# A two-block transformer on one core: weights' buffers moved by 64 bytes, later layers' inputs laid out 1024 bytes apart per feature tile

## The reference, cut to what matters

```
n = rmsnorm(h); proj = n @ w_in                       # qkv, iq, ak, av, aq, gates, z
merged = sig(gate_a) * (y_gdn @ w_branch_gdn) + sig(gate_b) * (y_dsa @ w_branch_dsa)
h = h + rmsnorm(merged @ w_out)
h = h + rmsnorm(square(relu(rmsnorm(h) @ w_up)) @ w_down)
x = x + rmsnorm(retention(rmsnorm(x), a_w_in, a_w_out))
x = x + rmsnorm((silu(g) * u) @ w_down0)              # [g, u] = conv3(rmsnorm(x) @ w_up0)
k, v = rmsnorm(x) @ w_kv
x = x + rmsnorm(diff_attention(rmsnorm(x), k, v, w_q, ...))
x = x + rmsnorm((silu(g) * u) @ w_down1)
```

## Time and profile before

| | us |
|---|---|
| median of three runs | 1258.31 |
| the profiled execution | 1258.36 |
| its span in the trace | 1256.6 |
| TensorE busy | 1240.9 |
| VectorE busy | 920.2 |
| ScalarE busy | 698.9 |
| granted clock of TensorE, mean | 0.998 of full speed |

### The profile page before, as it was taken

One profiled execution on the slowest core, in us unless ns is written; L12 is line 12 of the kernel. 1 busy time (PEld: TensorE's weight loads), 2 busy tenths in 40 slices (PEclk: granted clock), 3 DMA queues, 4 the chain that ended last, 5 costly groups with the idle time before them and its releaser, 6 DMA issues.

```text
span 1256.6 us, 23318 instructions
## 1 busy us (share of the span) xinstructions
PE 1240.9 (99%) x9036; PEld 1163.5 (93%) x9036; DVE 920.2 (73%) x1294; ACT 698.9 (56%) x1082; POOL 166.0 (13%) x113
## 2 busy tenths in 40 slices
PE   8999999999999999999999999999999999999998
PEld 7997999999989998889998989999889998999986
DVE  8786874878768775457734557999758777999954
ACT  6556465654446443445354646666557567766652
POOL 0000142000000000000000001663200000465310
PEclk9999999999999999999999999999999999999999
DMA  8452333311365545555553455545565444455562
GB/s 319 162 175 101 135 135 101 135 68 68 140 213 185 191 177 201 191 179 185 182 208 111 149 186 168 195 173 198 193 227 176 161 153 166 168 178 189 183 238 98
DMA packets 30316, 212.46 MB, mean 169 GB/s; under 512 B 3488, under 2 KB 3616, under 8 KB 5280
## 3 DMA queue, kind: packets, MB, share of 16 engines
q1 hardware_dynamic: 29088, 206.15, 46.9%
q0 software_dynamic: 1152, 5.24, 1.2%
HBM read 210.33 MB, written 1.05 MB: 168 GB/s over the span
## 4 chain that ended last, share of the span: by engine, by line
PE 90%; DVE 6%; ACT 3%; issue 1%; DMA 0%; DVEq 0%; SPq 0%; ACTq 0%
PE lin L541 52%; PE lin L707 21%; PE lin L568 2%; PE lin L2928 2%; DVE wlo L514 1%; PE lin L570 1%; ACT whi L507 1%; PE aux L2672 1%; PE aux L2644 1%; PE aux L730 1%; PE lin L2351 1%; PE aux L2530 1%; PE aux L2790 1%; PE aux L2600 1%; PE aux L2476 0%
## 5 line engine op out<-in xcount | busy, mean ns | idle before, releaser
L514 DVE TENSOR_TENSOR wlo<-raw,whi 128x2048 fp32r<-128x2048 f32 x183 | 424.6, 2323 | 163.4 <-ACT whi L507 162.8
L507 ACT CAST whi<-raw 128x2048 fp32r<-128x2048 f32 x192 | 365.1, 1905 | 175.4 <-DMA raw<-in_stream 145.8
L541 PE MATMUL lin<-xhi,whi 128*128 128x256 f32 (+2 forms) x1584 | 451.1, 285 | 1.9 <-DVE ctmp L1657 1.9
L541 PE MATMUL lin<-xlo,whi 128*128 128x256 f32 (+2 forms) x1584 | 447.3, 282 | 0.0
L541 PE MATMUL lin<-xhi,wlo 128*128 128x256 f32 (+2 forms) x1584 | 446.8, 282 | 0.0
L541 PEld LDWEIGHTS lin<-xhi,whi 128*128 128x128 f32 x1584 | 299.8, 189 | 3.7 <-issue 2.5
L541 PEld LDWEIGHTS lin<-xhi,wlo 128*128 128x128 f32 x1584 | 300.0, 189 | 0.0
L541 PEld LDWEIGHTS lin<-xlo,whi 128*128 128x128 f32 x1584 | 298.4, 188 | 0.4
L871 POOL TENSOR_TENSOR fu<-fs,ft 128x256 f32<-128x256 f32 x44 | 98.8, 2246 | 258.3 <-ACT fs L1485 258.3
L2311 DVE SCALAR_TENSOR_TENSOR ft<-fy,par,ft 128x254 f32<-128x254 f32 (+1 forms) x176 | 112.4, 678 | 5.9 <-DVE ft L2311 0.2
L541 PE MATMUL lin<-whi,xhi 128*128 128x256 f32 x256 | 73.9, 289 | 0.0
(11 more groups left out here) (463 smaller groups left out, 2163.3 us busy)
## 6 DMA issues: line engine op xcount, KB each, us to landing
raw<-in_stream SPq DMA_DIRECT2D x192, 1024.0 KB, 4.9
gp<-in_gains POOLq DMA_DIRECT2D x6, 512.0 KB, 3.9
c<-in_const SPq DMA_DIRECT2D x1, 1460.0 KB, 15.6
h<-in_x SPq DMA_DIRECT2D x2, 544.0 KB, 4.2
c<-in_const POOLq DMA_DIRECT2D x1, 1024.0 KB, 6.6
ht<-in_xtok POOLq DMA_DIRECT2D x1, 1024.0 KB, 9.7
raw<-in_stream SPq DMA_DIRECT2D x1, 640.0 KB, 6.4
out<-ht SPq DMA_DIRECT2D x1, 512.0 KB, 2.6
```

The costliest lines, as they stand in the source:

```text
L507: nc.scalar.copy(whi[:, s0 % 4], raw[:, s0 % 4]).then_inc(hi_ready, 1)
L514: nc.vector.tensor_tensor(wlo[:, s0 % 4], raw[:, s0 % 4], whi[:, s0 % 4].bitcast(F32), ALU.subtract).then_inc(lo_ready, 1)
L541: ins = nc.tensor.matmul(out, a, b, start=start and n == 0, stop=stop and n == 2)
```

## The change

The weights' buffers begin 64 bytes later. `ones` moves up behind them; nine small tensors become slices of one tensor `few` without padding, so that everything behind ends 128 bytes earlier than before (B is 93056). From the end of the first block's mixing on, the inputs of a layer no longer use the 272-column tiles: `xs_of` has for each of the five layer boundaries its own view of the same place, with 256 columns per tile (1024 bytes) and its own start, XAT bytes further on. No instruction is added or taken away, and no wait.

```diff
+WAT = 64
+XAT = {"mlp": 0, "ret": 64, "ffn0": 64, "diff": 0, "ffn1": 128}
...
-        raw = at("raw", 0, [P, RAW_N, KT, NCOL])
-        wlo = at("wlo", 0, [P, RAW_N, KT, NCOL], F32R)
-        whi = at("whi", 32768, [P, RAW_N, KT, NCOL], F32R)
-        par = at("par", 65536, [P, NPAR])
-        cursor = [65536 + 4 * NPAR]
+        raw = at("raw", WAT, [P, RAW_N, KT, NCOL])
+        wlo = at("wlo", WAT, [P, RAW_N, KT, NCOL], F32R)
+        whi = at("whi", WAT + 32768, [P, RAW_N, KT, NCOL], F32R)
+        ones = at("ones", WAT + 65536, [P, P])
+        par = at("par", WAT + 66048, [P, NPAR])
+        cursor = [WAT + 66048 + 4 * NPAR]
...
-        ones = nxt("ones", [P, P])
-        eps = nxt("eps", [P, 3])
+        few = nxt("few", [P, 75])
+        eps, gcum, ktsc, rcol = few[:, 0:3], few[:, 3:20], few[:, 20:29], few[:, 29:31]
+        ss, bs, rc, s2 = few[:, 31:35], few[:, 35:37], few[:, 37:39], few[:, 39:41]
+        bcg = few[:, 41:75].rearrange("p (n c) -> p n c", c=17)
...
         xhi = at("xhi", B, [P, KT, T1], F32R)
         xlo = at("xlo", B + 8704, [P, KT, T1], F32R)
+        xs_of = {name: tuple(at(f"{part}_{name}", B + 8704 * n + o, [P, KT, SEQ], F32R) for n, part in enumerate(("xhi", "xlo")))
+                 for name, o in XAT.items()}
...
-                nc.scalar.activation(xhi[:, kt, c * P:c * P + P], turned_tile(kt, c), ACT.Copy,
+                nc.scalar.activation(xs_of[pre][0][:, kt, c * P:c * P + P], turned_tile(kt, c), ACT.Copy,
...
-            pe_post_layer(pe, "wout", xhi, xlo, "mlo", KT, lambda end: end // 2, pre="mlp")
-            pe_layer("up", xhi[:, :, 0:SEQ], xlo[:, :, 0:SEQ], lead=4, pre="mlp")
+            pe_post_layer(pe, "wout", *xs_of["mlp"], "mlo", KT, lambda end: end // 2, pre="mlp")
+            pe_layer("up", *xs_of["mlp"], lead=4, pre="mlp")
...
-            x_hi, x_lo = xhi[:, :, 0:SEQ], xlo[:, :, 0:SEQ]
+            x_hi, x_lo = xs_of["ret"]
...
-                xh, xl = (x2hi, x2lo) if name == "dq" else (x_hi, x_lo)
+                xh, xl = (x2hi, x2lo) if name == "dq" else xs_of["diff"]
...
-            pe_layer(f"fu{k}", xhi[:, :, 0:SEQ], xlo[:, :, 0:SEQ], lead=2, pre=f"ffn{k}")
+            pe_layer(f"fu{k}", *xs_of[f"ffn{k}"], lead=2, pre=f"ffn{k}")
```

More of the change, by code:

```diff
@@ L171, in program @@
         gtmp = nxt("gtmp", [P, 3, 3, 8])
-        bcg = nxt("bcg", [P, 2, 17])
-        gcum = nxt("gcum", [P, 17])
-        ktsc = nxt("ktsc", [P, 9])
         egl = nxt("egl", [P, 8])
@@ L183, in program @@
         rstd = nxt("rstd", [P, T1])
[L184 to L188, removed]
         gqn = nxt("gqn", [P, 2, 8])
@@ L1026, in act_body @@
                     act.wait_ge(S("merged"), j + 1)
-                    nc.scalar.copy(xhi[:, 2 * j:2 * j + 2, 0:SEQ], merged[:, 2 * j:2 * j + 2]).then_inc(S("mhi"), 1)
+                    nc.scalar.copy(xs_of["mlp"][0][:, 2 * j:2 * j + 2], merged[:, 2 * j:2 * j + 2]).then_inc(S("mhi"), 1)
                     load_hi(FIRST[name] + j + 3, 0)
@@ L1552, in low @@
                 a = slice(c * P, c * P + P)
-                nc.vector.scalar_tensor_tensor(xlo[:, kt, a], turned_tile(kt, c), pcol(PRE_GAIN[pre], kt),
-                                               xhi[:, kt, a].bitcast(F32), ALU.mult, ALU.subtract)\
+                nc.vector.scalar_tensor_tensor(xs_of[pre][1][:, kt, a], turned_tile(kt, c), pcol(PRE_GAIN[pre], kt),
+                                               xs_of[pre][0][:, kt, a].bitcast(F32), ALU.mult, ALU.subtract)\
                     .then_inc(S("xlo"), 1)
@@ L1825, in dve_body @@
                 dve.wait_ge(S("mhi"), j + 1)
-                nc.vector.tensor_tensor(xlo[:, a, 0:SEQ], merged[:, a], xhi[:, a, 0:SEQ].bitcast(F32), ALU.subtract)\
+                nc.vector.tensor_tensor(xs_of["mlp"][1][:, a], merged[:, a], xs_of["mlp"][0][:, a].bitcast(F32), ALU.subtract)\
                     .then_inc(S("mlo"), 1)
@@ L2935, in out_part @@
                     ins.then_inc(S("tile_postdiff"), 1)
-            pe_token_pair("diff", x_hi, x_lo)
+            pe_token_pair("diff", *xs_of["diff"])
             project("dk", 0)
```

## The result

The changed kernel took 1263.91 us (six runs, 1260.82 to 1265.74) against 1258.37 (six runs of the kernel before, 1256.81 to 1258.65): ratio 1.0043, 95% interval 1.0033 to 1.0053. It is slower by 5.5 us; the forecast was 8.6 us faster. The profiled execution of after took 1265.74 us (span 1263.9), 7.3 us of span more than the one of before, and it is also the slowest of the six.

A forecast was written before the change was run, and what follows sets the result against it. TensorE was taken as the bound, its time a count of matmuls times a pace. Terms −1.4 − 2.5 − 1.2 − 3.0 − 0.5 = −8.6 us took the median 1258.31 to 1249.8; range 1238 to 1262, forecast's own 1243 to 1255.

The forecast's parts named there:

- the one on 512 columns: Six 512-column layers, M−S to 192: all at 226.7 ns, 0 for 1200 matmuls and −0.5 us for `wout`.
- the nearer row: Timeline row of `down`, 512 columns at constant M−S 0, 226.7 ns; taken as the pace at 192.
- its four rows: Timeline paces of `up` 118.3, `dq` 120.0, `down` 226.7 and `wout` 231.7 ns, said to differ only in operand places.
- Rival 3: 512-column layers stall at M−S 192: 1256.3 us, or 1261.9 at 236 ns; chance 0.13 for 1255 to 1262.
- rival 1: Evenly spaced 256-column layers settle at 120.0 ns, +7.3 us, total 1265; chance 0.13 for 1262 to 1265.
- M−S 128: `rq`, `rk`, `rv`, `rg`, `ret`'s token pair and `fu0`: from 118.3 to 117.5 ns, −0.8 ns a matmul.
- `fu1` at 192: 1008 matmuls of `fu1` go to 113.3 ns; with VectorE limiting, −3.0 us instead of the whole 5.0.
- the 240 matmuls at 192: Stationary-input matmuls in `dv` and the tiled slot of `up`: −5.0 ns each, −1.2 us.
- rival 4: Throughout the kernel distance does nothing and paces come from something else: 1258.4 us, chance 0.09.
- M−S 64: `wbd`, `wbg`, `dq` from 120.0 to 117.5 ns, −1.4 us; `up` beyond its tiled slot and `dk` from 118.3 to 117.5.
- The cap by VectorE in `fu1`: At 113.3 ns a `fu1` slot takes TensorE 5.44 us but VectorE 5.61, limiting the gain to −3.0 us.
- the free lag: In `fu1` VectorE may fall up to 2.5 us behind, 0.17 a slot, before TensorE waits; ten slots taken.

The follow-up runs named there:

- the first two experiments: Two variants of the changed kernel: M−S of 512-column layers back to 0, inputs' distances kept, 1254.72 us; inputs left 1088 bytes apart, 1263.67 us.
- the first experiment: Changed kernel with B padded so M−S of most 512-column layers is 0 again, XAT raised by 64 to keep the inputs' distances; 1254.72 us.
- the fifth kernel: Changed kernel with B padded so most 512-column layers stand at M−S 0, and XAT 192 for all inputs; 1249.71 us, ratio 0.9938.

## Why the prediction was wrong

**The step that failed** is the one on 512 columns: "I take 226.7 for all, the nearer row: it too has one distance throughout, and 192 is the one that did best with 256 columns." Its terms were 0 and −0.5 us; these layers measured +7.6 and +0.4. That is 8.5 us of the 14 between forecast and result. The nearer row was near in its tile spacing and not in M−S, the very quantity that the argument had just named; and a ranking from 256 columns was carried to 512, where it is turned round: 0 is best (226.7) and 192 worst (233.3). The prediction had called the place of the operands the one thing in which its four rows differ; they differ in columns as well. Rival 3 came true, with "From 233.3 on it eats the whole gain": all six layers came to 233.3 to 233.4. That the total, 1263.9, lies in the band of rival 1 (1262 to 1265) and above that of rival 3 is chance: of rival 1 only `rq` and `rk` at 120.0 came, and rival 3 had reckoned with the full gain of the other layers.

**The three smaller misses.** M−S 128 was taken at 117.5 from six matmuls in a row; where a layer stays there it settles at 118.7 or at 120.0: +1.2 us over 2160 matmuls instead of −1.7. (The caution in rival 1, that six may be too few, held for this distance.) `fu1` at 192 settled at 117.7 and not at 113.3: −0.7 instead of −3.0. And the 240 matmuls at 192 gave 0.6 in `dv`, half of what was put down. In each of these a distance was given one settled pace, where the experiments show two.

**What held.** TensorE bounds the kernel, the waits of TensorE that the traces list grew only from 9.2 to 10.7 us, and distance sets the pace: rival 4 is refuted by the first two experiments (226.8 and 233.3 ns for the same instructions). With it goes what I had taken from the rule of the Trainium skill ("TensorE: Matmul & The Clock Gate", "Step-by-step: what each phase is for") that loading weights takes no bandwidth from the running matmul: that no distance would matter. Whether it is the load that holds up the matmul, no run shows. M−S 64 gave 117.4 and 117.8 in `wbd` and `dq` (forecast 117.5), and 117.6 and 117.8 in `up` and `dk`. Packing cost nothing that shows.

**The cap by VectorE in `fu1`** could not act in after, where a slot takes TensorE 48 × 117.7 = 5.65 us. VectorE's timeline there, its first operation of a slot and, two slots on, again:

```profile
1129.21 0.68 DVE L2302 TENSOR_TENSOR fy<-lin,rstd 128x512 f32<-128x512 f32 x1
1129.81 2.27 DVE L513 TENSOR_TENSOR wlo<-raw,whi 128x2048 fp32r<-128x2048 f32 x1
...
1140.44 0.68 DVE L2302 TENSOR_TENSOR fy<-lin,rstd 128x512 f32<-128x512 f32 x1
```

5.62 us a slot, as before. In the first experiment `fu1` did enter at 113.3, and the forecast of that step can be read there. All matmuls in two stretches of 30 us:

```profile
1080.00:1110.00 30.00, 30.00 (x267) 30.00 (x267) 29.13 (x34) 19.59 (x29) 18.96 (x12) 1.00 0.53 183
1130.00:1160.00 30.00, 30.00 (x257) 30.00 (x256) 29.28 (x33) 20.28 (x28) 19.56 (x11) 1.00 0.51 175
```

Between them VectorE's lag behind a slot's last matmul had grown from 1.15 to 2.55 us, and the head of a slot came late. VectorE:

```profile
1116.54 0.68 DVE L2302 TENSOR_TENSOR fy<-lin,rstd 128x512 f32<-128x512 f32 x1
1117.14 2.27 DVE L513 TENSOR_TENSOR wlo<-raw,whi 128x2048 fp32r<-128x2048 f32 x1
```

and TensorE:

```profile
1119.26 0.28 PE L540 MATMUL lin<-xlo_ffn,whi 128*128 128x256 f32 x1
1119.37 0.28 PE L540 MATMUL lin<-xhi_ffn,wlo 128*128 128x256 f32 x1
1119.55 0.38 PE L540 MATMUL lin<-xhi_ffn,whi 128*128 128x256 f32 x1
```

The split ends at 1119.41, the slot that wants it starts at 1119.55, 0.18 us after the matmul ahead instead of 0.11; one slot later the split ends at 1125.05 and the slot starts at 1125.19, 0.14 us behind it again. After nine slots the free lag, forecast at up to 2.5 us, is spent. I had 14 slots for a start without lag and took ten; the layer began with 1.15 us of lag and added 0.17 a slot, as forecast. The chain of the stretch says the same, share by line, first for the first experiment:

```profile
by line: DVE ft L2310 33.1%; DVE wlo L513 23.5%; issue 20.1%; DVE fy L2302 9.8%; PE lin L567 2.9%; PE lin L569 2.0%; DVEq L2310 1.8%; PE lin L2927 1.6%; PE aux L729 1.2%; PE lin L540 1.1%; DVEq L134 0.6%; DVEq L2305 0.6%; DVEq L122 0.6%; DV
```

and for after:

```profile
by line: PE lin L540 93.6%; PE lin L567 2.9%; PE lin L569 2.1%; PE aux L729 1.0%; PE lin L580 0.4%; PE aux L762 0.2%; issue 0.0%
```

What was not forecast: after two late heads the layer goes on at 117.7, as though entered anew (in `fu0` of the fifth kernel after five). In all `fu1` was 2.3 us shorter than before, against 3.0 forecast.

**What stays open.** Why 512 columns are best at the distance at which 256 are worst; what in the chip has the period of 256 bytes; what picks one of the two paces. That the spread of a kernel's runs (1252.0 to 1257.6 in the first experiment) is this choice made anew in each execution fits the traces and was not shown: there is one profile for each kernel. The clock that falls near 28 us in some executions and not in others is a second source, worth 1.6 us between the profiles of before and of the first experiment.

## What to carry to other kernels

When a kernel is bound by a pace, take the pace from starts and set it against the quantity that the change moves, here the difference of the two operands' addresses; a row counts as near only if that quantity is the same in it, and a ranking found for one width must be measured again for another. A short stretch at one value (six matmuls) does not tell where a long one settles. Move one group of buffers at a time: here the inputs' half, well placed, was worth 7 to 11 us, and the weights' half, from which 1.4 us of gain were forecast, cost 5.5 to 6.

## What the runs showed of the hardware

Settled paces in ns from start to start, at full clock, by M−S modulo 256; two numbers are two paces at which different executions or layers settled and stayed:

| columns | 0 | 64 | 128 | 192 |
|---|---|---|---|---|
| 256 | 120.0 | 113.3 or 117.7 | 118.7 or 120.0 | 113.3 or 117.7 |
| 512 | 226.7 | 229.0 or 233.3 | 232.4 | 233.3 |

Once settled, a pace lasts for hundreds of matmuls; in `fu1` of the first experiment it changed after two late slots. That the first steps of a layer make the choice is what the traces suggest; it was not shown. Other distances than these four were tried in no run.
